# Seven half-size block products in the feed-forward of an encoder layer, with weight sums made by GpSimd in the stages before

## What is computed

```
h = RMSNorm(x);  [qa|ka|va|qb|kb|vb] = h @ w_in             # 1024 x 2304
mixer A: 8 heads of 64, own chunk of 64 and 8 before, QK-norm, learned bias by distance
mixer B: 8 heads over 2 key heads, own chunk and 2 before, QK-norm, rotary, sinks
x = x + concat(A, B) @ w_out                                # 1024 x 1024
gate, up = split(RMSNorm(x) @ w_gate_up)                    # 1024 x 2816 each
y = silu(causal conv of width 3 over tokens (gate) + bias) * up
x = x + y @ w_down                                          # 2816 x 1024
```

## Time and profile before

| what | us |
|---|---|
| median of three runs | 2730.96 |
| the profiled execution | 2730.9 |
| its span, first to last instruction | 2729.1 |
| TensorE busy | 2604.4 (95%) |
| DVE busy | 1376.9 (50%) |
| ScalarE busy | 887.8 (33%) |
| GpSimd busy | 189.9 (7%) |
| mean granted clock of TensorE | 0.978 |
| moved by DMA | 271.61 MB, mean 100 GB/s |

### The profile page before, as it was taken

The page is one execution under the profiler, slowest core; times in us unless marked ns, Lnnn a source line. Parts: engine busy times, 40 slices in busy tenths (PEclk is TensorE's granted clock), DMA queues, the critical chain, the costliest instruction groups (busy, mean ns, idle before and its releaser), DMA issues.

```text
span 2729.1 us, 45154 instructions
## 1 busy us (share of the span) xinstructions
PE 2604.4 (95%) x16553; PEld 2504.4 (92%) x16553; DVE 1376.9 (50%) x2973; ACT 887.8 (33%) x1696; POOL 189.9 (7%) x125
## 2 busy tenths in 40 slices
PE   6999999589999979969999999999999999999998
PEld 3888888489999979859999999999999999999998
DVE  5544444466667645565534552554355346625651
ACT  4233332476777633232212221221122222212220
POOL 0000000332322200000000002000000210000000
PEclk8999999799999989979999999999999999999999
DMA  6232231544334165562221223322122342221221
GB/s 218 86 96 79 92 94 48 123 114 102 86 86 101 46 236 180 192 238 66 73 75 55 69 92 121 123 69 79 60 69 71 105 145 65 79 68 62 69 87 64
DMA packets 175286, 271.61 MB, mean 100 GB/s; under 512 B 19138, under 2 KB 120482, under 8 KB 175074
## 3 DMA queue, kind: packets, MB, share of 16 engines
q1 hardware_dynamic: 167842, 246.13, 29.8%
q0 software_dynamic: 4848, 23.12, 2.4%
q10 hardware_dynamic: 2512, 1.26, 0.2%
HBM read 216.35 MB, written 55.69 MB: 100 GB/s over the span
## 4 chain that ended last, share of the span: by engine, by line
PE 55%; DVE 0%; DMA 0%; POOL 0%; issue 0%; ACT 0%; SPq 0%; POOLq 0%
PE ffn_z L81 55%; DVE ffn_h_lo L1646 0%; DMA ffn_acc<-h2T_scratch 0%; ACT ffn_h_hi L1592 0%; POOL yT L1537 0%; POOL gate_sample L1542 0%; DVE ffn_acc L1703 0%; POOL gate_prompt L1543 0%; SPq L1488 0%; SPq L1486 0%; POOLq L1541 0%; POOLq L1536 0%
## 5 line engine op out<-in xcount | busy, mean ns | idle before, releaser
L81 PE MATMUL ffn_z<-ffn_h_hi,ffn_w_hi 128*128 128x352 f32 x2112 | 680.6, 322 | 22.1 <-DVE ffn_w_lo L1641 21.9
L81 PE MATMUL ffn_z<-ffn_h_lo,ffn_w_hi 128*128 128x352 f32 x2112 | 680.2, 322 | 0.0
L81 PE MATMUL ffn_z<-ffn_h_hi,ffn_w_lo 128*128 128x352 f32 x2112 | 680.0, 322 | 0.0
L1583 ACT ACTIVATE ffn_w_hi<-ffn_w_raw 128x1024 fp32r<-128x1024 f32 (+1 forms) x180 | 205.6, 1142 | 716.9 <-PE ffn_z L81 715.8
L81 PEld LDWEIGHTS ffn_z<-ffn_h_hi,ffn_w_hi 128*128 128x128 f32 x2112 | 397.2, 188 | 24.2 <-DVE ffn_w_lo L1641 23.0
L81 PEld LDWEIGHTS ffn_z<-ffn_h_hi,ffn_w_lo 128*128 128x128 f32 x2112 | 397.5, 188 | 0.0
L81 PEld LDWEIGHTS ffn_z<-ffn_h_lo,ffn_w_hi 128*128 128x128 f32 x2112 | 397.5, 188 | 0.0
L81 PE MATMUL ffn_z<-ffn_y_lo,ffn_w_hi 128*128 128x352 f32 x1056 | 340.0, 322 | 0.0
L81 PE MATMUL ffn_z<-ffn_y_hi,ffn_w_hi 128*128 128x352 f32 x1056 | 339.7, 322 | 0.0
L81 PE MATMUL ffn_z<-ffn_y_hi,ffn_w_lo 128*128 128x352 f32 x1056 | 339.5, 321 | 0.0
L242 PE MATMUL project_z<-project_w_hi,project_h_hi 128*128 128x512 f32 (+3 forms) x680 | 255.3, 375 | 13.0 <-DVE project_w_lo L411 12.9
(11 more groups left out here) (149 smaller groups left out, 3790.8 us busy)
## 6 DMA issues: line engine op xcount, KB each, us to landing
ffn_w_raw<-w_gu SPq DMA_DIRECT2D x132, 512.0 KB, 3.6
ffn_w_raw<-w_dn SPq DMA_DIRECT2D x48, 704.0 KB, 4.1
combine_w_raw<-w_o SPq DMA_DIRECT2D x24, 512.0 KB, 4.9
combine_o_raw<-oT_scratch SPq DMA_DIRECT2D x12, 704.0 KB, 6.4
combine_x<-xT SPq DMA_DIRECT2D x12, 704.0 KB, 7.4
x1T_scratch<-combine_x SPq DMA_DIRECT2D x12, 704.0 KB, 7.5
ffn_acc<-x1T_scratch POOLq DMA_DIRECT2D x3, 2816.0 KB, 11.8
yT<-ffn_acc POOLq DMA_DIRECT2D x24, 352.0 KB
```

The costliest lines, as they stand in the source:

```text
L81: last = nc.tensor.matmul(out, w_parts[w](k), act_parts[a](k), start=(k == 0 and (w, a) == PASSES[0]), stop=(k == n_k - 1 and (w, a) == PA ...
L1583: nc.scalar.activation(w_hi[s][:, 0:n_k, :], w_raw[s][:, 0:n_k, :], ACT.Copy).then_inc(w_hi_ok[s], 1)
```

## The change

**The feed-forward.** Two 2x2 block matrices are multiplied with seven block products and 15 additions in place of eight products (the form of Winograd). The weights are cut into B11, B12, B22, B21 (left and right tile by upper and lower half of the inner dimension), the activations into A11, A12 (upper and lower half of the inner dimension for the first 352 tokens) and A21, A22 (the same for the second). A group is two output tiles (gate and up of 128 features, or two tiles of the down projection) for one token block, and its seven products are:

| product | activations | weights | TensorE's bank |
|---|---|---|---|
| 1 | A11 | B11 | x |
| 6 | S2 = S1 - A11 | T2 = B22 - T1 | x, on top of 1 |
| 7 | S3 = A11 - A21 | T3 = B22 - B12 | x, on top |
| 4 | A22 | T4 = B21 - T2 | x, on top |
| 2 | A12 | B21 plain | y |
| 5 | S1 = A21 + A22 | T1 = B12 - B11 | z |
| 3 | S4 = A12 - S2 | B22 plain | z, on top of 5 |

ScalarE or DVE read bank x between these products (`keep`, `add_x`), and DVE adds the rest (`evict`). Gate/up groups have four inner steps, down groups two, and one (in the first of six parts of the features) where the part has two tiles. The order interleaves products 4 and 3 of a group with products 1, 6, 7 of the next (`ffn_schedule`). All is straight-line code: 138 groups, 966 products.

**The weights.** Products 1, 2 and 3 take plain blocks: loaded, and split by ScalarE and DVE in the stage, as before. Products 4 to 7 take weight sums, which come from DRAM already as hi and lo, 512 KB for a gate/up product, 256 KB for a down one.

**GpSimd.** The sums T1 to T4 and their hi and lo are made in 132 pieces (`WeightSums.piece`): 68 in `project`, after all of its own weights are split, 42 in `attend`, between its own three operations of a tile, 22 in `combine`. Each stage ends only when its pieces are stored. A new input w_quads holds the four blocks of each piece side by side.

**The sums of the activations.** For the input of the next block GpSimd makes S1 to S4 and passes them through DRAM (`sums`, `load_h`), ScalarE and DVE split them in the last four down groups. For the first block DVE and GpSimd do it at the start. For the gated result, DVE makes S1 to S4 and seven lo parts, ScalarE seven hi parts, once for every two gate/up groups.

**In `project`** the norm's gain is put on the weights (ScalarE's scale, and a scalar_tensor_tensor on DVE, in 40 halves of pieces) and no longer on x; three tiles become two or are reused; the first tile's transposes move behind the second tile's first matmuls; SP loads x ahead of the stores. In `attend` the last tiles of GpSimd's loop are unrolled and the cache is split in two parts.

```diff
+class WeightSums:
...
+    def piece(self, n):
+        pool, at = self.nc.gpsimd, n - self.first
+        hi, lo = (self.parts[at % 3][:, a] for a in range(2))
+        four = lo.bitcast(F32)
+        b11, b12, b22, b21 = t1, t3, t2, t4 = tuple(four[:, j, :] for j in range(4))
+        pool.wait_ge(self.ld[at % 3], 16 * (at // 3 + 1))
+        pool.tensor_tensor(t1, b12, b11, ALU.subtract).then_inc(self.sum_ok, 1)
+        pool.wait_ge(self.sum_ok, 4 * at + 1)
+        pool.tensor_tensor(t3, b22, b12, ALU.subtract).then_inc(self.sum_ok, 1)
...
+        self.load(n + 2)
+        pool.wait_ge(self.sum_ok, 4 * at + 4)
+        pool.tensor_copy(hi, four).then_inc(self.hi_ok, 1)
+        pool.wait_ge(self.hi_ok, at + 1)
+        pool.tensor_tensor(lo, four, hi.bitcast(F32), ALU.subtract).then_inc(self.lo_ok, 1)
+        pool.wait_ge(self.lo_ok, at + 1)
...
+PREPARED = ((0, 68), (68, 110), (110, 132))
...
+        @block.gpsimd
+        def _(pool):
+            pool.wait_ge(w_lo_ok, KP * len(PIECES))
+            prep.begin()
+            for n in range(*prep_range):
+                prep.piece(n)
+            prep.stored()
...
+    for g, it in enumerate(groups):
+        late = g and not groups[g - 1]["flush"]
+        products.append((g, 1))
+        if late:
+            products.append((g - 1, 4))
+        products.append((g, 6))
+        if late:
+            products.append((g - 1, 3))
+        products += [(g, 7), (g, 2)]
...
+            def read_back(g, q):
...
+                if q == 1 and g > 1:
+                    old = groups[g - 2]
+                    pe.wait_ge(c21_gu_ok if old["kind"] == "gu" else c21_dn_ok, old["n"] + 1)
+                elif q == 6:
+                    pe.wait_ge(x_gu_rd if it["kind"] == "gu" else x_dn_rd, it["n"] + 1)
+                elif q == 7:
+                    pe.wait_ge(sum2_ok, g + 1)
+                elif q == 4:
+                    pe.wait_ge(sum3_ok, g + 1)
+                elif q == 2 and g > 1:
+                    pe.wait_ge(c11_ok, g - 1)
+                elif q == 5 and g > 1:
+                    pe.wait_ge(c12_ok, g - 1)
+                elif q == 3:
+                    pe.wait_ge(c22_ok, g + 1)
...
+            for c, (g, q) in enumerate(products):
+                it = groups[g]
+                evict(g, q, c)
...
+                if q == 5 and it["kind"] == "dn":
+                    add22(g)
+                if q == 3 and it["kind"] == "dn":
+                    add12(g)
+                if q == (2 if it["flush"] else 5) and it["kind"] == "gu":
+                    first_half(g)
+                if q == 6 and waiting:
+                    second_half(g - 1)
+                if q == 7 and waiting:
+                    times(g - 1, 0)
+                    times(g - 1, 1)
+                if q == 7 and unit_after(g) is not None:
+                    sums_of_unit(unit_after(g))
...
+                if q in SPREAD and unit_after(g) is not None:
+                    split_unit(unit_after(g), SPREAD[q])
+                if h_due(g, q):
+                    low_h(it["b"] + 1, *h_due(g, q))
+                for n in due.get(c, ()):
+                    low_w(n)
```

1020 lines of the change are left out of this document (701 added, 319 removed).

## The result

The changed kernel takes 2799.38 us (median of 4 runs) against 2730.26 for the kernel before (4 runs): a ratio of 1.0246, 95% interval 1.0231 to 1.0261. It is **slower by 2.5%**, where 2630 us were predicted, and above the end of the range (2775). The profiled execution took 2798.86 us (span 2796.7).

A forecast was written before the change was run, and what follows sets the result against it. The prediction took TensorE to bound the kernel, with DVE, GpSimd and DMA partly idle: 2730.9 - 188.8 (matmuls) + 46 (feed-forward) + 32 (projection) + 8 (attention) + 2 (output projection) = 2630 us, range 2560 to 2775.

The forecast's parts named there:

- the cost of a piece beside the projection: GpSimd in the projection: 6.8 us a piece, 5.5 to 8.5; 68 pieces end at 514 us, +32 us.
- GpSimd is in time: Projection and attention: at 6.3 us a piece the projection ends at 480 us, total 2588 us; chance 0.23.
- The rival with DVE: Projection and attention: DVE holds GpSimd up, 0.75 us a hit, kernel slower, 2780 to 2840 us; chance 0.13.
- Attention, +8 predicted: Attention: GpSimd's 28.7 us a tile exceeds the 28.3 us period; +8 us, between -2 and +70.
- Feed-forward, +46 predicted: Feed-forward: saved TensorE time lost to DVE, 16 + 14 + 16 us, together +46 us (10 to 130).
- The matmul term: Feed-forward: 8316 matmuls instead of 9504 at 0.159 us each, -188.8 us, the ceiling of the gain.
- Heavy groups, 16 us: Feed-forward, every second gate/up group: DVE's 13.1 us against TensorE's 13.35; 0.5 us stall in each of 33, 16 us.
- The start, "stays as it is": Feed-forward's start: first DMA at 1196.30, TensorE begins at 1209.54, behind loads and first splits before and after; no cost.
- Half-size groups, 14 us: Feed-forward, 12 small down groups: DVE's 4.5 us against TensorE's 3.34, 12 x 1.2 = 14 us.
- The next block's input, 16 us: Feed-forward, last four down groups of blocks 0 and 1: splits make 8.6 us a group against 6.67, 16 us.
- The third rival: Feed-forward: DVE's order costs 3 us per heavy group, 1 us per down group; 2745 us, half 2688; chance 0.12.
- the sign that I gave for a wrong 46 us: Feed-forward: TensorE waiting for DVE (additions to sums, evictions) by more than 100 us in total.

The follow-up runs named there:

- late_load: Against the changed kernel: each piece's load of the piece two ahead issued after the last subtraction instead of before the copy; 2691.65 us, 0.9865 of before.
- moves_only: The kernel after the change with each piece's six operations left out except in the first three pieces of each stage, loads and stores kept; 2690.80 us (1 run).
- no_small_groups: late_load with the twelve half-size down groups, 252 matmuls, left out; 2636.78 us (1 run).
- plain_first: late_load with a plain block's load in the feed-forward issued up to three products ahead of the loads of sums; 2689.21 us.
- no_next_input: late_load without the splits and loads of the second and third block's input, these blocks using the first block's; 2681.57 us (1 run).
- last_unit: late_load with a block's last unit summed and split in the order the last down groups use it; 2696.16 us.

## Why the prediction was wrong

**The step that failed** is the cost of a piece beside the projection: I worked it out as issue and operation times with waits for the instruction before, 6.8 us, and took GpSimd's load as an issue that waits for nothing. It waits for a store. I had the store's landing only at the very end (4 us once); in truth a wait for it stands in 65 of the 68 pieces. I had named the point of break-even, 7.8 us, and blamed the port for the case beyond it. The piece took 7.66, and all the rest was dearer, so the sum turned. Moving the load alone turns it back (late_load, 2691.65). The wait isn't the whole of the miss: late_load is still 62 us above the forecast. There the first three stages together are 26 us shorter than I had them, and the feed-forward 84 longer, whose start and block ends I had put at nothing.

By the parts of the piece (means of 68, profile after):
- Four subtractions: estimated 1.88, measured 2.01 (0.46 undisturbed). Subtraction of 512 columns 1.28, measured 1.31. The copy 0.7, measured 0.69 (0.62 in the row shown). Load's issue 0.55, measured 0.56. Store's 0.91, measured 1.04. Together 5.32 against 5.60: the bounds from near rows served well.
- Waits for the instruction before: estimated 5 x 0.30. Measured 0.08 between two operations, and 0.34 only ahead of the store: 0.7 together with all small gaps. The row I took 0.30 from the earlier trace rows stood ahead of a DMA. So this term was 0.8 too high and hid half of the missing wait.
- Wait for the store: estimated 0, measured 1.4, which with the others makes 7.66.

So with most of the wait gone the piece is 6.26 us (late_load): the rival "GpSimd is in time" would have been right on the projection, at the 6.3 us and 480 us that it names (482.9 measured). Its 2588 us would not, for the feed-forward's sake. And without GpSimd's work the projection ends 6 us earlier than before, not the 14 that I gave as the most.

**The shared port.** The rival with DVE had the outcome on its side and not the cause. This case's hit is there: a subtraction of 128 columns beside DVE's subtraction of 1024 with two inputs, first GpSimd's row, then DVE's, kernel after:

```profile
313.91 1.39 POOL L135 TENSOR_TENSOR project_quads<-project_quads 128x128 f32<-128x128 f32 x1
```

```profile
313.75 1.23 DVE L483 TENSOR_TENSOR project_h_lo<-project_x_raw,project_h_hi 128x1024 fp32r<-128x1024 f32 x1 [2.84 <-ACT project_h_hi L381]
```

0.46 became 1.39. The Trainium skill, "SBUF — State Buffer", section "Who interferes with whom", says such a pair excludes each other; by that rule the trace agrees. But over all 68 pieces the six operations took 4.00 us in the mean against 3.72 in attention's 42 pieces: 0.3 us a piece, 20 us of GpSimd, where the rival's average was 0.5 to 0.8 and the slower case two hits.

**Attention, +8 predicted, +15.7.** 28.7 against a period of 28.3 us was the right comparison, with the wrong piece: in the kernel after 12 waits for a store take 45.4 us of GpSimd there. With the load moved attention still takes 4 to 8 us more than without pieces, and moves_only shows 6.7 with the sums left out: traffic, which I had costed at nothing.

**Output projection, +2 predicted, +15.8.** I checked only that 150 us of GpSimd fit in 232. They do; the 22 pieces cost 10 to 14 us by their traffic, about 6 of them in the first 31 us, where the stage's own loads fill the DMA engines.

**Feed-forward, +46 predicted over the matmuls, +130 measured** (1474.4 - 1532.8 + 188.8).
- The matmul term is right: 0.159 us in every undisturbed stretch.
- Heavy groups, 16 us: measured next to nothing. 1005 matmuls in 160 us, with DVE at 68%: the lump of 5.8 us is hidden. The long stretches between half-size groups and block ends, 6048 of the 8316 matmuls, lose 8.4 us in late_load, 6.8 of them in one block.
- The start, "stays as it is": the first matmul came 11.4 us behind the stage's first DMA, before 6.7, and then starved. The first 87 us lose 37.0 us in late_load, where the kernel before lost 9.9. So +27. I had also read the earlier trace rows wrongly: the chain's last link begins at 1209.54 us, but TensorE's first matmul of the stage stands at 1203.00.
- Half-size groups, 14 us: 28.6 when left out (no_small_groups), 32.3 by place, a part of it the loads' order (plain_first).
- The next block's input, 16 us: 18.6 (no_next_input), 13.9 of it at the two block ends where it stands.
- Block ends, beyond that input not charged: 59.9 us, of which the kernel before had 9. The 17 us shown above for late_load hold 39 matmuls, 6.2 us of work, so 10.8 are lost in them alone. The three ends are alike: 18.6, 19.3 and 22.0 us.
- The first four groups of the second and third block, not charged: 12.1 us.
- 27 + 32.3 + 50.9 + 12.1 + 8.4 make the 131 us. So the places are all known. What stays open is the division by cause: in late_load about 100 of the 150 us are idle time of TensorE, and the other 50 matmuls that came further apart, most of them at the lower clock (the 10 us from 1683 us hold 23 matmuls at a granted clock of 0.50, the next 10 hold 59 at 0.99). Which wait is to blame for which part of the lower clock, no run shows.

**Two more things in the prediction.** The third rival's sum takes my 16 us off twice: its terms make +131, so 2761 us and not 2745. And the sign that I gave for a wrong 46 us, more than 100 us of waits for DVE, didn't show: in the kernel after they add up to 73 us, a part of that ahead of the stage, since waits alone don't hold what the clock takes.

## What to carry to other kernels

When a loop is costed by its instructions, follow each buffer round the ring as well: a load that stands early in an iteration waits for the store issued at the end of the last one, and here a store that landed 4.4 us after its issue began, with 3.3 us of issue and work to cover it, decided the sign of the whole change. Moving the load behind the arithmetic was enough here; a fourth buffer would be the other cure, and no run tried it. When an edit's gain is as small as the scatter of a stage, look whether the time came back at the place that was edited: last_unit's didn't. Work "beside" a stage is free only if it is free in engine time, in DMA share during the stage's first loads, and in its place in the queue, and each is to be looked up apart.

## What the hardware showed that I had not expected

- A dependent GpSimd operation starts 0.08 us after the one before; a DMA issue that waits for the same engine's operation starts 0.30 us after it (1.0 at most).
- GpSimd's store of 512 KB takes 4.0 us in the median to land beside the projection and 5.5 beside the output projection, counted from the start of its issue, the range being 2.9 to 9.7; its issue takes 1.04. In late_load, where stores follow each other faster, it was 4.6 and 6.3.
- In late_load TensorE had no matmul from 1679.8 to 1683.0 us; from 1683 to 1693 us the granted clock was 0.50 to 0.52 (1.2 GHz), with matmuls 0.29 us apart where 0.16 is usual. 78 matmuls without use at the block ends gave the useful ones there 4.8 us back, and 40 at the start nothing.
- A small DMA behind four large ones held ScalarE for 5.94 us while it was being issued (6.04 in the kernel after); on GpSimd's queue, issued later, it took 0.56.
